# Hybrid decoder trunk on one core: the adaLN conditioning as unsplit fp32 products with the weights stationary, and the unit evacuations on one engine

## What is computed

```
sc  = silu(c)                        # c: 1 prompt row and 8 sample rows, 9 rows in all
mod = sc @ w_ada + b_ada             # w_ada 1024 x 6144; six parts of 1024: sh_m sc_m gt_m sh_f sc_f gt_f
h   = rms_norm(x) * (1 + sc_m) + sh_m
u   = h @ w_in + b_in                # 1024 x 2048: GLU value, GLU gate, recurrent, gelu gate
ya  = silu(layer_norm(causal_dwconv31(value * sigmoid(gate))))
yb  = rg_lru(causal_dwconv4(recurrent)) * gelu(gelu gate)
x   = x + gt_m * (concat[ya, yb] @ w_out)
x   = x + gt_f * (relu((rms_norm(x) * (1 + sc_f) + sh_f) @ w_up)^2 @ w_down)
y   = rms_norm(x)                    # and the conv and recurrence states as further outputs
```

## Time and profile before

| what | us |
|---|---|
| median of 3 runs | 1296.06 |
| the runs | 1296.06, 4485.14, 1294.8 |
| the profiled execution's own time | 1296.5 |
| its span, first to last instruction | 1294.7 |
| PE busy in it | 1192.5 |
| mean granted clock | 0.957 |

### The profile page before, as it was taken

The page is one execution under the profiler, slowest core; times in us unless marked ns, Lnnn a source line. Parts: engine busy times, 40 slices in busy tenths (PEclk is TensorE's granted clock), DMA queues, the critical chain, the costliest instruction groups (busy, mean ns, idle before and its releaser), DMA issues.

```text
span 1294.7 us, 16511 instructions
## 1 busy us (share of the span) xinstructions
PE 1192.5 (92%) x6175; PEld 1068.0 (82%) x6175; DVE 723.8 (56%) x809; ACT 402.8 (31%) x704; POOL 369.3 (29%) x217
## 2 busy tenths in 40 slices
PE   6798999999723999899999999999999999999996
PEld 2687999997423888888998998998988988988985
DVE  2649699996686455524534534535535435435447
ACT  4752334433791433420320320320310310311322
POOL 0246777652453010410320410410410311311300
PEclk9697999999966999899999999999999999999998
DMA  9533343321204110210210210310300300201102
GB/s 298 163 98 98 98 126 117 109 86 49 68 32 151 37 33 1 82 50 1 78 53 1 81 49 0 90 40 0 97 32 0 97 32 10 87 32 32 49 33 105
DMA packets 74661, 87.26 MB, mean 67 GB/s; under 512 B 3816, under 2 KB 53248, under 8 KB 74627
## 3 DMA queue, kind: packets, MB, share of 16 engines
q1 hardware_dynamic: 72448, 85.21, 21.1%
q10 hardware_dynamic: 2179, 1.61, 0.5%
HBM read 81.72 MB, written 5.08 MB: 67 GB/s over the span
## 4 chain that ended last, share of the span: by engine, by line
PE 85%; DVE 5%; SPq 2%; ACT 2%; POOL 2%; DMA 1%; issue 1%; ACTq 0%; DVEq 0%; POOLq 0%
PE ps L1472 15%; PE ps L1474 14%; PE ps L1473 14%; PE ps L1614 11%; PE ps L1615 11%; PE ps L1617 11%; PE ps L1480 1%; PE ps L1621 1%; PE ps L1620 1%; SPq L265 1%; PE ps L1365 1%; PE ps L1364 1%; DVE tmp_a L1235 1%; DMA x<-in_x_prompt 1%; DVE ga L1232 1%
## 5 line engine op out<-in xcount | busy, mean ns | idle before, releaser
L1472 PE MATMUL ps<-act_hi,w_hi 128*128 128x384 f32 (+1 forms) x1152 | 381.0, 331 | 8.0 <-DVE act_lo L1048 3.9
L1473 PE MATMUL ps<-act_lo,w_hi 128*128 128x384 f32 (+1 forms) x1152 | 378.4, 328 | 0.0
L1474 PE MATMUL ps<-act_hi,w_lo 128*128 128x384 f32 (+1 forms) x1152 | 378.3, 328 | 0.0
L1472 PEld LDWEIGHTS ps<-act_hi,w_hi 128*128 128x128 f32 x1152 | 218.7, 190 | 11.0 <-issue 4.8
L367 POOL TENSOR_TENSOR wb_lo<-raw,wb_hi 128x1024 fp32r<-128x1024 f32 x40 | 99.9, 2506 | 430.0 <-ACT wb_hi L568 403.3
L367 POOL TENSOR_TENSOR w_lo<-raw,w_hi 128x1024 fp32r<-128x1024 f32 x48 | 118.4, 2468 | 363.8 <-ACT w_hi L568 305.7
L1272 DVE TENSOR_TENSOR ps<-ps,gt_p 128x1024 f32<-128x1024 f32 x72 | 88.7, 1233 | 237.6 <-PE ps L1617 237.6
L1473 PEld LDWEIGHTS ps<-act_lo,w_hi 128*128 128x128 f32 x1152 | 218.8, 190 | 1.6
L1474 PEld LDWEIGHTS ps<-act_hi,w_lo 128*128 128x128 f32 x1152 | 218.6, 190 | 0.0
L1614 PE MATMUL ps<-wb_hi 128*128 128x512 f32 x512 | 199.4, 389 | 1.1 <-ACT gt_s L899 1.1
L1615 PE MATMUL ps<-wb_lo,wb_hi 128*128 128x512 f32 x512 | 199.2, 389 | 0.0
(11 more groups left out here) (224 smaller groups left out, 1298.9 us busy)
## 6 DMA issues: line engine op xcount, KB each, us to landing
raw_ada<-in_w_ada SPq DMA_DIRECT2D x32, 512.0 KB, 3.7
raw<-in_w_up SPq DMA_DIRECT2D x32, 512.0 KB, 4.0
raw<-in_w_down SPq DMA_DIRECT2D x32, 512.0 KB, 3.3
ada<-in_w_ada SPq DMA_DIRECT2D x8, 1024.0 KB, 15.0
x<-in_x_prompt SPq DMA_DIRECT2D x16, 512.0 KB, 8.8
raw<-in_w_in SPq DMA_DIRECT2D x16, 512.0 KB, 4.8
raw<-in_w_out SPq DMA_DIRECT2D x8, 512.0 KB, 3.4
out<-x SPq DMA_DIRECT2D x8, 512.0 KB, 2.6
```

Source lines behind the costliest of these rows:

```text
L1472: mm(out, wh, xh, start=(k == 0), stop=False)
L1473: mm(out, wh, xl, start=False, stop=False)
L1474: last = mm(out, wl, xh, start=False, stop=(k == KD - 1))
```

## The change

- Every group is computed in plain fp32 with the weights stationary: for each 128 columns of the group, eight products (one per 128 rows of w_ada) of a 128x128 block against the 9 moving columns of `c_t`. A group is 32 such products. The result is already turned, so the splits, the row copies, `pick`, `stk`'s first use and the turning products go, on every engine.
- Groups 0 to 3 are `ada_first`; group 2 stands ahead of units 0 to 3, group 3 behind them. DVE adds the bias for 16 rows of `mod` at once (`modulation`), three times in all.
- Groups 4 to 7 are `ada_piece`s in steps 1 to 4 (step 0 and steps 5 to 7 have none). Groups 8 to 11 (`late_group`) stand in the gate section, one behind the gate products of each round. Their weights are loaded into `ada_late`, which shares its place with `w_hi` and `w_lo`, so from the end of step 7; each quarter is loaded again when it has been used, with a w_out transfer between two groups.
- DVE waits for the last late group, for `modulation(32, 48)`, behind `gated_input(3)` and ahead of the scans. The last state transpose stands behind the last late group.
- `xsq` moves from `tmp_b` to `lru`, the variances get three banks of their own, `squares(0)` moves into the last gelu step, and `w_out_hi(0)` behind the deviations.
- ACT scales all 16 units; DVE keeps the even units' high and low parts.
- The loads of `ada0` are cut by columns (1 KB pieces) where they were cut by rows (2 KB pieces). SP's loops over the steps are written out.

```diff
-            def ada_plain(g):
+            def ada_first(g):
+                for i in range(4):
+                    if i % 2 == 0:
+                        pe.wait_ge(ada0_in[g][i // 2], 16)
+                    at = P + 36 * g + 9 * i
+                    for k in range(KD):
+                        last = mm(ps[:, 0, at:at + 9], ada0[:, g, k, i * P:(i + 1) * P], c_t[:, k, :],
+                                  start=(k == 0), stop=(k == KD - 1))
                 last.then_inc(ada0_used, 1)
+            def ada_piece(a, i):
+                w, done, n = (ada_step, ada_in, a + 1) if a < ADA_S else (ada_late, late_in, a - ADA_S + 1)
+                bank, at = 6 + a // ADA_S, 36 * (a % ADA_S) + 9 * i
+                pe.wait_ge(done[i], 16 * n)
+                for k in range(KD):
+                    last = mm(ps[:, bank, at:at + 9], w[:, i, k, :], c_t[:, k, :],
+                              start=(k == 0), stop=(k == KD - 1))
+                last.then_inc(ada_used, 1)
...
+            ada_first(2)
+            pe.wait_ge(sa_cp, 2)
+            for u in range(4):
+                turn_unit(u)
+            ada_first(3)
...
-            def step(m, last=False, late=()):
+            def step(m, last=False, group=None):
...
-                        if c == 0 and s == 0:
-                            for i in late:
-                                ada_piece(m - 1, i)
-                            group_turn(m + ADA0 - 1, 7, 0)
-                        for i in ((), (2 * s,), (2 * s + 1,))[c]:
-                            ada_piece(m, i)
+                        if group is not None and c > 0:
+                            ada_piece(group, 2 * s + c - 1)
...
-            turn_state(1, 7, 4 * (KA - 1), lambda j: tail_a[:, j, 0:120])
-            recurrent_gates(0)
+            late_group(ADA_S)
+            turn_state(1, 6, 4 * (KA - 1), lambda j: tail_a[:, j, 0:120])
+            recurrent_gates(1)
+            late_group(ADA_S + 1)
             turn_state(2, 6, 4 * (KA - 1), lambda j: tail_a[:, j, 120:240])
+            recurrent_gates(2)
+            late_group(ADA_S + 2)
             pe.wait_ge(tails, 2)
-            turn_state(3, 7, KB - 1, lambda j: tail_bp[:, j, :])
-            recurrent_gates(1)
+            turn_state(3, 6, KB - 1, lambda j: tail_bp[:, j, :])
+            recurrent_gates(3)
+            late_group(ADA_S + 3)
             turn_state(4, 6, NB * (KB - 1), lambda j: tail_b[:, j, :])
...
+            for a in range(ADA_S, ADA_G - ADA0):
+                for i in range(4):
+                    load_ada(a, i)
+                load_out(a - ADA_S + 2)
...
+            dve.wait_ge(ada_used, 8 * ADA_S)
+            modulation(32, 48, ps[:, 7, 0:144])
...
             for p in range(KD):
+                unit_full(2 * p + 1)
                 if p < KD - 1:
                     unit_full(2 * p + 2)
                 unit_high(2 * p + 1)
...
-            dve.wait_ge(ada_evac, ADA0)
+            dve.wait_ge(ada0_used, ADA0)
+            modulation(0, 16, ps[:, 0, P:P + 144])
```

More of the change, by code:

```diff
@@ L170, in trunk @@
         gf_in, stored = sem("gf_in"), sem("stored")
-        ada_in = [sem("ada_in0"), sem("ada_in1")]
+        ada_in = [sem(f"ada_in{i}") for i in range(4)]
+        late_in = [sem(f"late_in{i}") for i in range(4)]
         staged_out = sem("staged_out")
@@ L463, in _ @@
                     pool.wait_ge(st_tr, 3)
[L464 to L471, removed]
+                    pool.wait_ge(ada_evac, 2)
+                    sample_gate(0, M_GTM)
             pool.wait_ge(evac_a, 2 * J * NC)
@@ L572, in strip_hi @@
                 hi(n, slot, w_hi[:, slot, :], 16 * (n // 2 + 1))
[L574 to L589, removed]
-                act.activation(aw_hi[:, slot, :], raw_ada[:, slot, :],
-                               ACT.Copy).then_inc(ada_hi, 1)
-            def rows9(g):
-                act.wait_ge(ada0_used, g + 1)
-                act.activation(ada_rows[0:9, :], ps[0:9, 6 + g % 2, :], ACT.Copy).then_inc(rows_out, 1)
-            def ada0_high(e):
-                g, i = ADA_PLAIN + e // 4, e % 4
-                act.wait_ge(ada0_in[g][i // 2], 16)
-                wait(act, ada0_free, e - 3)
-                act.activation(ada_h[:, e % 4, :], ada0[:, g, 2 * i:2 * i + 2, :].rearrange("p a b -> p (a b)"),
-                               ACT.Copy).then_inc(ada0_hi, 1)
             def norm_x(t):
@@ L695, in gelu_out, with step @@
                           par[:, bass.ds(C_BIN + 3 * J + j, 1)], done)
-            def step(m, first, last, out_a, out_b):
-                if not first:
-                    wait_apart(act, ada_used, 4 * m)
-                    group_rows(m + ADA0 - 1, 6)
+            def step(m, last, out_a, out_b):
                 for c in range(NC):
-                    if c == 2 and not first:
-                        wait_apart(act, ada_tr, m + ADA0)
-                        group_out(m + ADA0 - 1, 7, 0)
                     wait_apart(act, strip_a, NC * m + c + 1)
@@ L765, in out_a, with out_b @@
                     gelu_out(c, bank, 2 * q, evac_a)
-                step(q + J + J // 2, False, last, out_a,
-                     lambda c, bank: gelu_out(c, bank, 2 * q + 1, evac_b))
+                def out_b(c, bank):
+                    if last and c == 2:
+                        squares(0)
+                    gelu_out(c, bank, 2 * q + 1, evac_b)
+                step(q + J + J // 2, last, out_a, out_b)
             with act.Fori(1, J) as j:
@@ L1078, in _ @@
             dve.tensor_scalar(hb[:, 1, :], par[:, C_BGX:C_BGX + J], 0.5, None, ALU.mult).then_inc(k_done, 2)
-            for e in range(4):
-                ada0_low(e)
             for h in range(2):
@@ L1541, in _ @@
             pe.wait_ge(sa_cp, 2)
-            pe.wait_ge(ada_evac, ADA0)
+            pe.wait_ge(ada_evac, 1)
             first_step()
-            step(1, late=(2, 3))
-            with pe.Fori(2, 2 * J - 1) as m:
+            for m in range(1, ADA_S + 1):
+                step(m, group=m - 1)
+            with pe.Fori(ADA_S + 1, 2 * J - 1) as m:
                 step(m)
             step(2 * J - 1, True)
-            group_turn(ADA_G - 1, 7, 0)
             pe.wait_ge(wg_in, 64)
@@ L1568, in recurrent_gates, with late_group @@
                            start=True, stop=True).then_inc(done, 1)
+            def late_group(a):
+                for i in range(4):
+                    ada_piece(a, i)
             for c in range(NC):
```

318 lines of the change are left out of this document (96 added, 222 removed).

## The result

The changed kernel takes 1323.09 us (median of 4 runs, 1322.96 to 1325.28), the kernel before 1296.48 on the same chip: a ratio of 1.0214, 95% interval 1.0194 to 1.0234 (a ratio of means, in which one run of the kernel before, of 4485.14 us, is left out). So it is slower, and whether by more than 2% the interval leaves open. The forecast was 1331, slower, with a range of 1284 to 1344. The shift of 26.6 us is all there when VectorE begins its first product behind the gates: 394.06 for 367.71, +26.35. The steps of the forecast can be read one after the other.

A forecast was written before the change was run, and what follows sets the result against it. PE was taken to bound the kernel (85% of the chain). Start +18, steps -13.7 and the gate section put DVE's first product at 402.0, not 367.71: 1296.5 + 34.3 = 1331 us, range 1284 to 1344.

The forecast's parts named there:

- The price: Narrow products on PE: 0.11 us an instruction at full clock, 7.0 a group; 0.2075 at half, 13.3 a group.
- Which clock: Runs of 64 narrow products on PE: claimed to go at half clock, read from two earlier stretches.
- Part (a): Start, up to the first strip: groups at half clock and units make it +18 us.
- Part (b): Steps 1 to 7: -13.7 us, steps 2 to 4 at 30.8 each, last strip ending at 320.9.
- rival 2: Steps: narrow pieces lower the clock there too, +12 us, 1343; chance 0.15.
- Part (c): Gate section, last strip to DVE's first product behind the gates: 402.0 against 367.71, +34.3 us.
- the full clock kept for a short while: Gate section: each late group in the three further rounds starts at full clock briefly, taking 11.5 us.
- Rival 1: Start and gate section: narrow runs get full clock everywhere, -12.1 us, 1284; chance 0.20.
- under about 10 us on average: Start and late groups: average time a group below which the kernel would be not slower.
- Rival 3: Start or gate section: one of the two keeps full clock, 1307; chance 0.15.

The follow-up runs named there:

- Run 2: Changed kernel with the four late groups moved behind the last gate products and the product that spreads the mixer's gate; 1307.63 us, ratio 1.0096.
- runs 4: Changed kernel with 128 moving columns (9 of conditioning, 119 zeros) in groups 0 to 3, same 64 instructions a group; 1302.51 us.
- run 6: Changed kernel with the four late groups' moving block repeated 14 times (126 columns for 9), place unchanged; 1308.3 us, ratio 1.0106.
- run 8: Changed kernel with only the first four groups' moving block repeated 14 times (126 columns for 9); 1301.03 us, ratio 1.0042.
- Run 9: Changed kernel with squares and roots of tiles 6 and 7 and scalings of tiles 4 to 7 ahead of the scale rows; 1323.25 us, ratio 1.0206.
- run 5: Changed kernel with VectorE scaling and shifting the odd activation units again, as before the change; 1327.04 us, ratio 1.0261.
- run 7: Changed kernel with 126-column moving blocks in first four and late four groups, late four behind the last gate products; 1269.24 us, ratio 0.9794.

## Why the prediction was right, and what was off

**The price.** 0.2075 at half clock and 0.11 at full were taken from eight narrow products. Measured: 0.215 in the runs of 64 at half clock, 0.106 in the pieces of 16 in the steps and in the fast part of the fourth group. Right.

**Which clock.** The step on which all hung was right: a run of narrow products is left at half. The two stretches it was read from could not show it by themselves: in each of them PE had also stood idle just ahead of the narrow products, 5.41 us and 1.34 us. The start of the changed kernel shows it in the pace alone, since the first change of clock on record there is a fall at 58.6 us and the clock column stands at 1.00 until then though an instruction takes 0.215 us. By the Trainium skill (TensorE: Matmul & The Clock Gate, Part 1, "What's actually happening") the clock follows how busy the engine has been; the trace does not agree for these products: PE and its loads were busy for 13.3 of 13.3 us in the third group, and its 64 instructions took 13.7 (the first of the stretches below). Run 2, where the clock falls inside an unbroken run, and runs 4, 6 and 8 are the other half of the proof: the same instructions with 126 or 128 columns go at full pace.

**Part (a).** Forecast: first strip at 84.6, +18. Measured: 84.35, +17.7, and that close by luck, since two errors cancel. The groups and transposes ended 2.3 us earlier (scales at 66.66, not 68.9), since behind the 16 transposes of units 0 to 3 the last group had the full clock for 3.3 us and took 10.5 for 13.3. The stretches of the changed kernel, the third group and the parts of the fourth (columns as above):

```profile
38.70:52.00 13.30, 13.30 (x64) 13.30 (x64) 4.21 (x5) 3.83 (x7) 2.46 (x1) 1.00 1.06 321
...
55.50:58.80 3.30, 3.30 (x31) 3.30 (x30) 0.00 (x0) 0.00 (x0) 0.00 (x0) 0.97 0.00 0
58.90:66.00 7.10, 7.08 (x34) 6.98 (x33) 0.00 (x0) 0.00 (x0) 0.00 (x0) 0.50 0.00 0
```

In 3.3 us 31 instructions, then 34 in 7.1. The units took 17.7 for 15.6. PE's two waits there end on VectorE's scalings of tiles 6 and 7, and VectorE had been waiting for ScalarE's roots of these tiles (timeline of DVE, changed kernel):

```profile
73.53 0.16 DVE L926 RECIPROCAL ssq<-ssq 128x1 f32<-128x1 f32 x1 [3.62 <-ACT ssq L526]
...
78.94 0.16 DVE L926 RECIPROCAL ssq<-ssq 128x1 f32<-128x1 f32 x1 [2.45 <-ACT ssq L526]
```

The change moved more than its description says: the squares and root of tile 6 and the scalings of tiles 4 to 6, which stood ahead of the scale rows, stand behind them now. I had counted both roots and tile 7's scaling. What I left out are ScalarE's own waits, 0.53 us for a low part on GpSimd and 1.44 us for one on VectorE, which stands in VectorE's order behind the scaling that waits for the root. So tile 7 came 1.1 us later than the 12.2 behind the scales that I had added up (one of the eight ScalarE scalings came after it), and the 21 transposes behind it took 4.4 us at half clock for 3.4. Run 9 shows that with the roots and scalings out of the stretch it takes 12.8, run 5 that ScalarE's larger share of the units is not what makes it long.

**Part (b).** Forecast: steps 2 to 4 at 30.8, last strip's end 320.9. Measured: 30.8, and 319.99 (the last product begins at 319.68 with 0.31). Step 1 took 32.5 for 33.4, from the first strip to it 32.0 for 31.6, steps 5 and 6 23.8 and 23.7 for 23.8. The 16 pieces of 1.69 keep the full clock between strips; rival 2 is out. Strips to last strip came to 235.6 for the 236.3 forecast.

**Part (c).** Gates at 329.87 for 329.0, right. Then the mis-sized term: the late groups. I gave them 10.3 + 3 x 11.5 = 44.8 us; they took 9.49 + 8.66 + 9.43 + 8.56 = 36.1, 8.7 less. The step that failed is "the full clock kept for a short while": I let the fast part end after 31 instructions in the first group, a number for which I gave no row, and, by the 11.5, after some 18 in the others; it lasted for about 39 and 47 of 64 (an estimate: those numbers of 0.106 with the rest at 0.215 give 9.5 and 8.6). The turn and gate products between, 6.6 forecast, took 6.7, 5.8 and 6.7. Behind the last group 4.5 us for 4.3. So 394.06 for 402.0, and 1323 for 1331.

**Rival 1** (full clock everywhere, 1284) is out by every group. Its sign, a group "under about 10 us on average", was too loose: the eight groups took 11.0 on average and the late ones alone 9.0, and the kernel is slower all the same. On a line between my own two ends, +34.3 us at 12.3 a group and -12.1 at 7.0, the change would be level near 8.4. Yet its arithmetic was nearly that of the wide blocks: it had the first strip at 62.6, and run 7, with the wide start, has it at 62.44.

**Rival 3** (half of it, 1307): neither place kept its clock, but each alone, once mended, gives just that: 1301 for the start (run 8), 1308 for the gate section (run 6).

## What to carry to other kernels

An instruction with fewer moving columns may cost more: before a product is narrowed, look in the trace for the same shape in a run and see at which clock it goes, and if at half, widen the moving block by repeating it (a stride of zero, no copy, and overlapping outputs in order, no more PSUM). Ask of a piece of work on the engine that bounds the kernel not only how long it is but whether the engine will be idle a little later: here the late groups' 256 instructions cost 26 us, narrow and between the gate products, and 383.85 - (341.94 + 40.5) = 1.4 us, wide and ahead of the output products. And when a wait ends on an engine, look at what that engine was waiting for: here PE waited for tiles that VectorE scales, and VectorE for ScalarE's roots of them, one of which had moved with the edit without being what the edit is about.

## What the runs showed of the hardware

- Fourteen times the columns took half the time: 64 fp32 matmul instructions with their loads in 13.7 to 13.8 us with 9 columns and, at the same place and with the same weights, in 7.3 to 7.4 with 126 or 128 (runs 4 and 8, from the second group on). At the full clock both widths cost about the same, 0.106 and 0.115. What the chip looks at when it grants the clock the runs don't show.
- Narrow products leave their clock to what follows: a round of 12 gate products took 4.9 to 5.8 us behind them and 3.8 behind wide ones (run 6), 3.82 before. Idle time does the same: in run 6 the clock was at 1.00 until PE's work ended at 380, and behind 39.7 us of idle time the output products took 0.63 us each for 3.5 us; in run 7, with no such gap, they took 0.39.
- The same 16 transposes were followed by the full clock in the changed kernel (10.67 for the group behind them) and not in run 9 (13.66): here the clock differed between two programs that are alike on PE up to that point, and 3 us hang on it.
- The clock column stands at 1.00 until the first change on record, a fall at 58.6 us in the changed kernel and at about 77 us in run 9. Until then the pace has to be read from the mean duration of an instruction.
